# HGRN2 and pooling block with SwiGLU: the mixers of the first two token tiles as one stage on shared weight loads

## What is computed

```python
u = rmsnorm(h, norm_mix_g)
q, f, i, og, xp, ga, gb = split(u @ w_in)          # 4 x 1024, 512, 2 x 1024 columns
# branch A, 8 heads of 128: f' = lb + (1-lb)*sigmoid(f); S = diag(f') S + (1-f') i^T; o = S^T silu(q)
ya = (rmsnorm_per_head(o) * sigmoid(og)) @ w_br_hgrn
# branch B: for 4 groups of 128 channels, trailing mean over 2, 4, 8, 16 tokens minus the token, then a group matmul
yb = (pool(xp) @ w_pool_grp * pool_scale) @ w_br_pool
h = h + (sigmoid(ga) * ya + sigmoid(gb) * yb) @ w_out
u = rmsnorm(h, norm_ffn_g)
h = h + (silu(u @ w_ffn_gate) * (u @ w_ffn_up)) @ w_ffn_down      # 2816 wide
out = rmsnorm(h, final_norm_g)[:, 16:]
```

## Time and profile before

| what | us |
| --- | --- |
| three runs | 2166.81, 2477.38, 2167.08; median 2167.08 |
| the profiled execution, as timed | 2170.29 |
| its span on the slowest core (5) | 2168.7 |
| spans of the 8 cores | 2158.5 to 2168.7 |
| TensorE (PE) busy | 2088.9 (96% of the span) |
| VectorE (DVE) busy | 1001.8 (46%) |
| ScalarE (ACT) busy | 1007.0 (46%) |
| GpSimd (POOL) busy | 574.0 (26%) |

### The profile page before, as it was taken

One profiled execution on the slowest core, in us unless ns is written; L12 is line 12 of the kernel. 1 busy time (PEld: TensorE's weight loads), 2 busy tenths in 40 slices (PEclk: granted clock), 3 DMA queues, 4 the chain that ended last, 5 costly groups with the idle time before them and its releaser, 6 DMA issues.

```text
span 2168.7 us, 38075 instructions; the slowest of 8 cores (2158.5 to 2168.7 us)
## 1 busy us (share of the span) xinstructions
PE 2088.9 (96%) x11476; PEld 1106.8 (51%) x11476; DVE 1001.8 (46%) x1756; ACT 1007.0 (46%) x1492; POOL 574.0 (26%) x671
## 2 busy tenths in 40 slices
PE   6777998999999999999999999999999999999997
PEld 3432554555555555555555555555555555554447
DVE  4644453447534742474246523662357235732223
ACT  4832763258415742464247623662358324731111
POOL 3121120001105251423243143314332414223300
PEclk9988999999999999999999999999999999999999
DMA  9999999887565666557555755575557555565577
GB/s 202 211 198 249 217 223 238 228 213 221 147 183 154 186 190 177 158 156 225 170 151 170 223 162 159 168 222 162 166 164 199 180 173 158 165 175 174 169 197 191
DMA packets 232789, 405.24 MB, mean 187 GB/s; under 512 B 24208, under 2 KB 66704, under 8 KB 232592
## 3 DMA queue, kind: packets, MB, share of 16 engines
q1 hardware_dynamic: 210080, 364.62, 57.6%
q0 software_dynamic: 20880, 36.32, 11.7%
q10 hardware_dynamic: 1632, 1.88, 0.4%
HBM read 385.94 MB, written 53.08 MB: 202 GB/s over the span
## 4 chain that ended last, share of the span: by engine, by line
PE 84%; DMA 12%; SPq 1%; issue 1%; DVE 1%; ACT 1%; POOL 0%; DVEq 0%; POOLq 0%; ACTq 0%
PE psa L496 75%; DMA wsc<-wr 6%; DMA wr<-wpk 5%; PE psa L661 5%; DMA wr<-wsc 1%; PE psa L782 1%; SPq L364 1%; PE psa L796 1%; PE psa L815 1%; PE psa L816 1%; PE psa L831 0%; DMA fa<-xT 0%; PE psa L620 0%; PE psa L601 0%; DVE ba L630 0%
## 5 line engine op out<-in xcount | busy, mean ns | idle before, releaser
L496 PE MATMUL psa<-ba,wr 128*128 128x456 bf16 (+2 forms) x8960 | 1776.7, 354 | 19.8 <-DVE ba L546 6.6
L496 PEld LDWEIGHTS psa<-ba,wr 128*128 128x128 bf16 x8960 | 868.1, 98 | 830.2 <-issue 40.6
L906 DVE TENSOR_TENSOR ba<-psa,fa 128x456 bf16<-128x456 f32 (+1 forms) x198 | 124.5, 631 | 250.8 <-PE psa L496 213.0
L905 ACT ACTIVATE fa<-psa 128x456 f32<-128x456 f32 (+1 forms) x198 | 107.1, 551 | 217.1 <-PE psa L496 185.1
L589 POOL TENSOR_TENSOR fa<-fa 128x456 f32<-128x456 f32 (+1 forms) x160 | 158.0, 996 | 161.8 <-DMA fa<-xT 76.9
L773 POOL TENSOR_TENSOR ba<-fa 128x456 bf16<-128x456 f32 (+1 forms) x48 | 61.1, 1272 | 480.7 <-ACT fa L756 257.9
L363 POOL DMA_DIRECT2D wr<-wpk x145 | 76.8, 535 | 373.8 <-DMA wsc<-wr 180.6
L661 PE MATMUL psa<-wr,ba 128*114 128x512 bf16 (+1 forms) x576 | 136.6, 384 | 3.0 <-DMA wr<-wpk 3.0
L765 DVE TENSOR_TENSOR_SCAN fa<-ba,fa 128x456 f32<-128x456 bf16 (+1 forms) x72 | 83.4, 1159 | 120.1 <-ACT fa L763 120.0
L866 POOL TENSOR_TENSOR fa<-fa 128x456 bf16<-128x456 f32 (+1 forms) x48 | 55.3, 1152 | 289.2 <-DVE fa L863 289.2
L863 DVE SCALAR_TENSOR_TENSOR fa<-fa,psa 128x456 f32<-128x456 f32 (+1 forms) x72 | 45.3, 629 | 165.9 <-PE psa L496 165.9
(11 more groups left out here) (84 smaller groups left out, 1767.2 us busy)
## 6 DMA issues: line engine op xcount, KB each, us to landing
wr<-wsc SPq DMA_DIRECT2D x1040, 256.0 KB, 3.0
wr<-wpk POOLq DMA_DIRECT2D x128, 256.0 KB, 14.3
wsc<-wr SPq DMA_DIRECT2D x128, 256.0 KB, 18.3
wr<-wsc SPq DMA_DIRECT2D x72, 192.0 KB, 2.8
fa<-xT SPq DMA_DIRECT2D x6, 1824.0 KB, 13.9
outT<-fa SPq DMA_DIRECT2D x6, 1824.0 KB, 11.0
wr<-wsc SPq DMA_DIRECT2D x72, 128.0 KB, 2.3
fa<-xT SPq DMA_DIRECT2D x2, 1840.0 KB, 13.2
```

The lines of the kernel that those rows point to most:

```text
L496: last = e.matmul(ps[bank][:, 0:c1 - c0], lhsT=sl[0].ap(i * 128, (i + 1) * 128), rhs=s_.ap(c0, c1), start=(start and i == 0), stop=(stop a ...
L905: yield act(lambda e: e.activation(out=sg.ap(0, nt), in_=ps[bg][:, 0:nt], func=AF.Silu), [PS(bg)], [sg.rg(0, nt)], tset="S", banks=[bg])
L906: yield dve(lambda e: e.tensor_tensor(out=ACT[fc].ap(0, nt), in0=ps[bu][:, 0:nt], in1=sg.ap(0, nt), op=ALU.mult), [PS(bu), sg.rg(0, nt)], ...
```

## The change

The mixers of tiles 0 and 1 become one stage. `GROUP` lists the order of its 16 heads: (0,0), (1,0), (0,1), (1,1) and so on, as (tile, head). A weight unit has the name of tile 0 for both (`wkey`); it is loaded once and given back only after tile 1's product (`wdone`). `s_v` runs the value products of both tiles, `s_merge((0, 1))` both merges, those of tile 1 one and a half blocks behind (`GAP`), then WO of tile 0 and WO of tile 1. Tile 1 has its own buffers: `U2`, parts of `ACT`, `VB` and `H[2]`. The heads of this stage alternate between banks 6, 7 and banks 3, 4, each pair with a lock of its own, so 3 banks are left for other products until the last head; a fourth set of head buffers is added. The load of x for tile 1 has no gate any more. The feed-forward of tile 0 opens after the merges of both tiles (`mixed`, 1), and from tile 2 on the mixer of tile t opens after the merges of tile t-1, at first two tiles ahead of the feed-forward. The matmuls are the same in number and shape as before; 77 reloads, those of tile 1's mixer, are gone.

```diff
-        KA_, PN_, O_ = 6, 5, 6
+        KA_, KA2, PN_ = 6, 3, 5
...
+        HX = HALL[2]
+        class Mixer:
+            def __init__(self, u, v, go, yp, mix):
+                self.U, self.V, self.GO, self.YP, self.MIX = u, v, go, yp, mix
...
+        MAIN = Mixer(U, VB.sub(0, 4096), cut(GOB, 8), cut(YPB, 4), [Half(HS[0]["blk"], j * NTM, NTM) for j in range(8)])
+        TWIN = Mixer(U2, ACTB.sub(0, 4096), cut(ACTB, 8, 4096), cut(ACTB, 4, 4096 + 8 * NTM), cut(VB, 8))
...
-        free_banks = {b: 0.0 for b in range(NDENSE)}
+        free_banks = {b: 0.0 for b in range(KA2)}
...
+        GROUP = [[(t, h) for h in range(8) for t in (0, 1)]] + [[(t, h) for h in range(8)] for t in range(2, n_tiles)]
...
+        def wkey(t, name):
+            return (0, name) if t == 1 else (t, name)
+
+        def wdone(t, keys):
+            return () if t == 0 else keys
...
         def s_norm1(t):
             if t >= NH:
                 yield Gate(("stored", t - NH))
-            if t == 1:
-                yield Gate(("hs", 0, 7))
+            if t == 2:
+                yield Gate(("hs", 1, 7))
+                yield Count(("pooled", 0), 4)
+                yield Count(("pooled", 1), 4)
             yield from load_x(t)
...
         def s_head(t, h):
...
-            s = HS[(h + 1) % HSN]
-            thg = THG[h % 3]
+            grp, n = HSEQ[(t, h)]
+            KB = KA2 if t < 2 and n % 2 else KA_
+            s = HS[n % 4] if t < 2 else HS[(n + 1) % HSN]
+            thg = THGX[n % 4] if t < 2 else THG[n % 3]
...
+            if t < 2:
+                if n >= 4:
+                    yield Gate(("hs",) + grp[n - 4])
+            elif n >= 3:
+                yield Gate(("hs",) + grp[n - 3], ("head",) + grp[n - 3])
...
-            yield Lock("KA")
+            if t == 1:
+                yield Gate(("hs", 0, h))
+            yield Lock(f"KA{KB}")
...
-        def s_merge(t):
-            nt = SIZES[t]
-            yield Count(("head", t), 8)
-            yield Count(("pool", t), 4)
-            for j in range(8):
+        def s_merge(ts):
+            seq = [(t, j) for j in range(8) for t in ts]
+            gts = list(zip(GTA, GTB))
+            if len(ts) > 1:
+                gts = [(HS[1]["qs"], HS[1]["en"]), (HS[1]["th"], HS[1]["eb"])] + gts
+                seq = sorted(seq, key=lambda x: (x[1] + GAP * x[0], x[0]))
+            yield Gate(("hs", 1, 6)) if len(ts) > 1 else Count(("head", ts[0]), 8)
+            for m, (t, j) in enumerate(seq):
...
+            for t in ts:
+                nt, MIX = SIZES[t], MB(t).MIX
+                yield Count(("mix", t), 8)
+                hb = H[t % NH]
+                yield Spawn(0, s_norm2(t))
+                for j in range(8):
+                    b = yield Bank()
+                    yield mm(b, [wkey(t, f"WO{j}")], MIX, nt, done=wdone(t, [wkey(t, f"WO{j}")]))
...
         def s_ffn(t):
...
-            if t:
-                yield Gate(("downpe", t - 1))
+            yield Gate(("downpe", t - 1) if t else ("mixed", 1))
...
         def master():
-            for t in range(n_tiles):
-                if t >= 2:
+            yield Spawn(1, s_norm1(0))
+            yield Spawn(1, s_norm1(1))
+            yield Spawn(1, s_norm1(2))
+            yield Spawn(0, s_pool1(0))
+            yield Spawn(0, s_pool1(1))
+            yield Spawn(1, s_v([(0, 0), (0, 1), (1, 0), (1, 1)]))
+            for t, h in GROUP[0]:
+                yield Spawn(0, s_head(t, h))
+            yield Spawn(1, s_merge((0, 1)))
+            yield Spawn(5, s_ffn(0))
+            yield Spawn(5, s_ffn(1))
+            for t in range(2, n_tiles):
+                if t >= 3:
                     yield Gate(("oproj", t - 2))
-                yield Spawn(1, s_norm1(t))
-                if t:
-                    yield Gate(("mixed", t - 1))
...
```

More of the change, by code:

```diff
@@ L24 @@
 LAG = 8
+GAP = 1.5
 PG = 7
@@ L280, in build_nc @@
         NH = 3
[L281 to L282 removed]
+        HALL = [FA.alloc(8 * NTM) for _ in range(NH)]
+        H = [[b.sub(j * NTM, NTM) for j in range(8)] for b in HALL]
         CF = FA.alloc(C_TOT)
@@ L301, in build_nc @@
         RS = [FA.alloc(NTM) for _ in range(2)]
-        XP, SA, SB = (HS[2]["blk"].sub(i * XPW, XPW) for i in range(3))
         SG = [FA.alloc(NTM) for _ in range(2)]
@@ L524, in prologue @@
                 issue_load(0, u, s)
-            for i in range(HSN):
+            for i in range(HSN + 1):
                 g_(lambda e, i=i: e.memset(HS[i]["QI"].ap(128, 602), 0.0), [HS[i]["QI"].rg(128, 602)], dur=0.3)
@@ L644, in s_norm1 @@
                 yield Count(("u", t - 1), 8)
-            yield from norm(t, H[t % NH], P_G1, U, RSTD[0], "split" if t == 0 else "sum" if t >= POOL_FROM else "mm", apply_gate=Gate(("ufree", t - 1)) if t else None, out_flag="u")
-        def s_v(t):
-            nt = SIZES[t]
-            c = nt // 4
-            yield Count(("u", t), 8)
-            if t:
-                yield Count(("head", t - 1), 8)
-            for hf in range(2):
-                units = [(t, f"WI{hf}{i}") for i in range(4)]
+            yield from norm(t, H[t % NH], P_G1, MB(t).U, RSTD[0], "split" if t <= 1 else "sum" if t >= POOL_FROM else "mm",
+                            apply_gate=Gate(("ufree", 0 if t == 2 else t - 1)) if t >= 2 else None, out_flag="u")
@@ L655, in s_v, with fn @@
+        def s_v(parts):
+            for t, hf in parts:
+                nt = SIZES[t]
+                c = nt // 4
+                U_, V = MB(t).U, MB(t).V
+                yield Count(("u", t), 8)
+                if t == 2:
+                    yield Count(("res", 1), 8)
+                if t >= 3:
+                    yield Count(("head", t - 1), 8)
+                units = [wkey(t, f"WI{hf}{i}") for i in range(4)]
                 for ci in range(4):
                     b = yield Bank()
-                    def fn(e, sl, b=b, ci=ci):
+                    def fn(e, sl, b=b, ci=ci, c=c, U_=U_):
```

213 lines of the change are left out of this document (117 added, 96 removed).

## The result

The changed kernel takes 2206.59 us (median; 2205.26 to 2403.93, 4 runs) where the kernel before takes 2167.01 us (2166.81 to 2477.38, 4 runs) on the same chip: ratio 1.0181, 95% interval 1.0158 to 1.0204, slower by 1.8%. The interval is clear of 1 but reaches over 1.02, so slower is certain and slower by 2% is not. The forecast was 2130 us, faster. One of the four runs of each kernel (2403.93 and 2477.38 us) fell into a slower state of the chip, so ratios are of the other runs, and the span of the profile stands for an experiment that has too few of those.

What follows compares the result with a forecast made beforehand. PE is full after 440 us; 85 us are lost with tile 0, where weight loads wait on DMA. Work 2058 + lost 55 (heads, ACT-bound) + 4 (feed-forward 0) + 16 (tail) = 2133, timed and rounded 2130 us, range 2106 to 2154.

Steps and rivals of the forecast that it cites:

- I cost both together at nothing: Start, to the second head's norm matmul: tile 1's products and early x cost nothing (-3 to +6); 27 us lost, 95 us.
- ACT bounds this stretch: Second to last joint head's norm matmul: 96 us of ACT work at 0.88 busy takes 109 us; 55 lost by its end.
- Merges and WO: 0: Merges and WO of both tiles: PE-bound, 112 us of PE work against 96 of DMA, slots full; nothing lost.
- Feed-forward 0 beside mixer 2: 4: Stage of feed-forward 0 with mixer 2: DMA done 20 us ahead of PE, so 4 us lost, bounds 0 to 15.
- rival B: Slots and queue: units held for two tiles idle the DMA; feed-forward 0 with mixer 2 loses 25; 2152 us, chance 0.13.
- Later tiles: 0: Tile 3 onward: value products stand at the same place of PE's work as before; cost 0, bounds -1 to +5.
- Tail 16: End of the last tile: the same 16 us lost as before.
- A: Joint heads: ACT runs without gaps, 42 us lost, and the feed-forward loses nothing; about 2114 us, chance 0.22.
- C: Joint heads: PE's pauses keep its clock at the low level, 108 us lost; 2184 us, chance 0.05.
- E: Joint stage: tile 1's matmuls don't fill tile 0's DMA waits, only the reloads' DMA is saved; 2158 us, chance 0.04.
- D: Joint heads: each table change holds ACT twice as long, 44 us more; 2174 us, chance 0.01.

Runs made afterwards that it cites:

- run 14: Run 10 with tile 1's x load held on the chip until tile 0's last normalized chunk is there; span 2191.6 us.
- run 10: Changed kernel with tile 2's x load on ScalarE's queue, two norms off POOL, and a planner's gate on tile 2's first silu ahead of tile 3; 0.9998 of before.
- run 12: Changed kernel with one tanh of the forget gate done twice in each of the first sixteen heads; ratio to before 1.0242.
- run 13: Run 10 with the planner's price of a table change at 1.4 instead of 1.0 us during the joint stage; ratio to before 1.0027, span 2172.1 us.
- Run 1: Changed kernel with tile 2's x load issued from ScalarE's DMA queue instead of SP's; ratio to before 1.0129, span 2202.8 us.
- run 2: Changed kernel with norm 2 of tile 2 and norm 3 of tile 1 taken off POOL; ratio to before 1.0119, span 2193.8 us.
- run 6: Changed kernel with tile 2's x load on ScalarE's queue and the two norms off POOL together; span 2187.6 us (one run).
- Run 8: Changed kernel with a planner's gate that lets tile 3's mixer in only when tile 1's last norm is planned; ratio to before 1.0207, span 2223.6 us.
- run 11: As run 10, but with the planner's gate ahead of tile 3 on the second silu of tile 2; ratio to before 0.9997.

## Why the prediction was wrong

The forecast had 75 us lost, the profile has 147.3. The 72.3 between them, by the prediction's own steps:

- **"I cost both together at nothing", point at 95 us: +18.3.** It came at 113.2. The base was low: the 27 us lost at the first head's norm matmul were read on core 5 of the kernel before, which has the least of the eight (27 to 32, median 30.5). Of the 18.3, 7.5 are tile 1's x ahead of the weights (run 14 against run 10, 22.1 and 29.6 lost at the first value matmul; the step's own figure for it was 6.4). The rest is in PE's waits in 34 to 113 us, 8.1 in all (3.5 of them for a weight), and in its clock, 0.90 in 27 to 95 us. The value and pool products of tile 1 were said to fill DMA waits. At first they did not pay: by 76 us the changed kernel had started 37 us of matmul work and the kernel before 43, by 95 us 56 and 53, by 150 us 101 and 81 (medians of the cores). And they pushed the heads back: in 27 to 95 us ScalarE, the stage's later bound, is busy 37.88 us where the kernel before had 49.85, as the windows of the changed kernel and of the one before show:

```profile
27.00:95.00 68.00, 55.94 (x252) 29.52 (x251) 32.99 (x72) 37.88 (x58) 5.28 (x10) 0.90 0.74 152
```
```profile
27.00:95.00 68.00, 54.58 (x301) 29.69 (x298) 39.47 (x84) 49.85 (x73) 14.24 (x27) 0.97 1.06 211
```

- **"ACT bounds this stretch", 109 us: +6.6.** The work was sized well: 98.2 us of ScalarE for 96. The stretch took 115.5 us because the busy share was 85% for 88%: it was 90% and 92% in the first two windows below, and 62% in the last 25 us (15.37 of 24.70). As for the mechanism, run 12 bears it out for more work, and run 13 does not for less: other waits hold the stretch at the same length once ScalarE has less to do. Which ones stays open.

```profile
95.00:150.00 55.00, 48.65 (x288) 26.25 (x287) 38.31 (x80) 49.33 (x74) 8.21 (x16) 0.97 0.72 146
150.00:204.00 54.00, 41.04 (x267) 22.92 (x265) 42.71 (x87) 49.61 (x75) 5.00 (x10) 0.97 0.31 45
204.00:228.70 24.70, 18.18 (x98) 9.57 (x99) 16.70 (x38) 15.37 (x22) 0.00 (x0) 0.79 0.00 1
```

- **"Merges and WO: 0": +10.7.** "The slots are full when it begins" left out what stands in SP's queue. Tile 2's x, whose load has to wait for the last joint head, was never priced. Run 1 shows its size. By the medians of the cores the stretch from the last joint head to V2 loses 8.3 us in the changed kernel and 1.4 in run 1, so nearly the whole term is this load. On the slowest core of run 1 the stretch still loses about 8, with 4.3 us of waiting for this x.
- **"Feed-forward 0 beside mixer 2: 4", bounds 0 to 15: +20.7.** This failed most in kind. The step counted bytes, 20 us of cover, and not who issues them: POOL's two early norms, of which run 2 removes 17. It was rival B's size (25, chance 0.13) by another mechanism. The cover was not there either. The DMA engines were to have done 159 us of work by 204 us; they had done 0.65 x 204 = 133. With both queues free (run 6) the stage still loses 9.7 us, 5.6 of them in a wait for a reload. In the changed kernel too the DMA share is 1.02 ahead of 490 us:

```profile
362.10:490.00 127.90, 125.50 (x722) 68.09 (x721) 66.68 (x135) 75.49 (x111) 24.47 (x47) 1.00 1.02 223
```

- **"Later tiles: 0", bounds -1 to +5: +15.8.** The argument was that the same work stands at the same place of PE's order. That was read for V3 and V4 only (V8 stands 26 us of work earlier than before), and PE's order was not the question: on DVE norm 1 of the next tile had moved behind WO, with POOL at work beside it. Run 8 shows that the planned order is the cause (0.2 lost from V5 to V8), and runs 10 and 11 lose 3.8 and 4.9 from V3 to V8 with a gate that leaves no hole like run 8's.
- **Tail 16: right** (16.2).

What the shared loads are worth is little: run 6, with both queues free, is 12 us ahead of before at V2 (83.1 against 95.1), where the forecast had 40, and 2.5 at V3 (4.7 by the medians), where feed-forward 0 is behind both. Rivals: A fell (ScalarE had gaps). C did not come about: the clock was 0.97 in 95 to 204 us, and 0.79 only in the stage's last 25. E did not either: from 95 us on tile 1's products bring more matmul work than before had. D fell, as a row of the instruction groups in 95 to 204 us shows (seven loads, busy time, mean ns of one, idle before all seven):

```profile
L815 ACT ACT_TABLE_LOAD x7 | 9.0, 1283 | 0.1
```

In the Trainium skill, "ScalarE: Activation LUTs", What ACT_TABLE_LOAD costs, a drain of 1.38 us comes on top; the trace shows none.

A rule bears on run 1. In the Trainium skill, "Trainium Kernel Development and Optimization", Key Constraints, issuing DMAs from several engines "only saves the sequencer's issue time". By the rule the move would give back an estimated 0.4 us, the length of the issue (0.38 in the trace). Here one load moved from SP's queue to ScalarE's took 6.1 us off the time lost at V2 (7.5 by the medians), since 27 write-backs no longer stood behind its wait. The measurement decides.

What stays open: what bounds the joint heads once ScalarE has less to do, how the loss of the later tiles splits between the norm's place and POOL beside it, and whether any plan keeps run 6's lead at V2. Runs 10 and 11 lose it again between V2 and V3 (13 and 16 us), as run 6 loses 10. In run 10 PE waits 6.2 us there for reloads, between 440 and 500 us, with the DMA share at 1.06, so that work for the DMA engines which the joint stage left undone is a likely cause; no run tests it.
